# Two norms in a row: the second one's factor taken behind the projections it feeds

## The reference, cut to what matters

```python
h = layer_norm(DEEPNORM_ALPHA * h + swiglu_ffn(h, ...), ln_ffn_g[1], ln_ffn_b[1])   # end of the first block
...
h = rms_norm(x, norm_mix_g[0])        # x * rsqrt(mean(x * x) + 1e-6) * g
z = h @ w_in                          # even_mixer
u, v, q, k, vb = jnp.split(z, [512, 1024, 1536, 2048], axis=-1)
a_out = chunked_gmlp(jax.nn.gelu(u, approximate=False), jax.nn.gelu(v, approximate=False), ...)
qh, kh, vh = rms_norm(heads(q), q_g), rms_norm(heads(k), k_g), heads(vb)
```

## Time and profile before

| | |
|---|---|
| median of the runs | 2374.08 us |
| the profiled execution's own time | 2375.46 us |
| its span | 2373.8 us |
| PE busy | 2327.5 us (98%) |
| DVE busy | 1645.7 us (69%) |
| ACT busy | 1067.6 us (45%) |
| POOL busy | 326.8 us (14%) |
| the stretch of the change | 1232 to 1290 us of the span |

### The profile page before, as it was taken

The page is one execution under the profiler, slowest core; times in us unless marked ns, Lnnn a source line. Parts: engine busy times, 40 slices in busy tenths (PEclk is TensorE's granted clock), DMA queues, the critical chain, the costliest instruction groups (busy, mean ns, idle before and its releaser), DMA issues.

```text
span 2373.8 us, 36382 instructions
## 1 busy us (share of the span) xinstructions
PE 2327.5 (98%) x14683; PEld 2023.1 (85%) x14683; DVE 1645.7 (69%) x2191; ACT 1067.6 (45%) x1390; POOL 326.8 (14%) x295
## 2 busy tenths in 40 slices
PE   7799999999999999999999999999999999999999
PEld 7688899988886678999878779999887878899987
DVE  8835877746666778777486546999647655799942
ACT  6421544532336625446234453555523454455622
POOL 6402100002002340000123252000011002000000
PEclk9899999999999999999999999999999999999999
DMA  2432333233332123333333323332334212333332
GB/s 58 96 106 89 99 110 104 81 102 105 97 107 67 32 84 98 103 103 93 88 120 94 93 68 101 95 107 72 110 97 144 71 54 71 89 108 107 88 106 85
DMA packets 328908, 219.65 MB, mean 93 GB/s; under 512 B 11252, under 2 KB 319114, under 8 KB 328682
## 3 DMA queue, kind: packets, MB, share of 16 engines
q1 hardware_dynamic: 322362, 208.46, 29.7%
q0 software_dynamic: 3024, 7.90, 1.4%
q10 hardware_dynamic: 3360, 1.02, 0.2%
HBM read 206.59 MB, written 2.10 MB: 88 GB/s over the span
## 4 chain that ended last, share of the span: by engine, by line
PE 89%; DVE 5%; POOL 3%; ACT 2%; issue 1%; ACTq 0%; DMA 0%; SPq 0%; DVEq 0%; POOLq 0%
PE psum L1512 10%; PE psum L1514 10%; PE psum L1513 10%; PE psum L1259 9%; PE psum L1261 9%; PE psum L1260 9%; PE psum L1481 3%; PE psum L1482 3%; PE psum L1483 3%; PE psum L1680 1%; PE psum L1682 1%; PE psum L1681 1%; PE psum L1377 1%; PE psum L1373 1%; PE psum L1374 1%
## 5 line engine op out<-in xcount | busy, mean ns | idle before, releaser
L2272 ACT CAST w_hi<-w_stage 128x2048 fp32r<-128x2048 f32 x118 | 225.4, 1911 | 535.6 <-PE psum L1261 352.9
L3269 DVE TENSOR_TENSOR w_lo<-w_stage,w_hi 128x2048 fp32r<-128x2048 f32 x119 | 285.0, 2395 | 228.6 <-ACT w_hi L2272 228.5
L1512 PE MATMUL psum<-x_sum_hi,w_hi 128*128 128x256 f32 x1088 | 308.0, 283 | 0.0
L1513 PE MATMUL psum<-x_sum_lo,w_hi 128*128 128x256 f32 x1088 | 307.9, 283 | 0.0
L1514 PE MATMUL psum<-x_sum_hi,w_lo 128*128 128x256 f32 x1088 | 307.9, 283 | 0.0
L2342 ACT CAST w_hi<-w_parts 128x1024 fp32r<-128x1024 f32 x204 | 213.4, 1049 | 201.1 <-PE psum L1514 111.1
L3397 DVE TENSOR_TENSOR w_lo<-w_parts,w_hi 128x1024 fp32r<-128x1024 f32 x204 | 248.3, 1220 | 51.3 <-ACT w_hi L2342 50.1
L1259 PE MATMUL psum<-hidden_raw_hi,w_hi 128*128 128x512 f32 x594 | 232.1, 391 | 0.3 <-DVE w_lo L3269 0.3
L1261 PE MATMUL psum<-hidden_raw_hi,w_lo 128*128 128x512 f32 x594 | 231.1, 389 | 0.0
L1260 PE MATMUL psum<-hidden_raw_lo,w_hi 128*128 128x512 f32 x594 | 231.1, 389 | 0.0
L1512 PE MATMUL psum<-x_hi,w_hi 128*128 128x256 f32 x816 | 230.9, 283 | 0.0
(11 more groups left out here) (657 smaller groups left out, 5285.6 us busy)
## 6 DMA issues: line engine op xcount, KB each, us to landing
w_stage<-in_ffn_w_down_dram SPq DMA_DIRECT2D x64, 704.0 KB, 4.7
w_parts<-in_ffn_w_gu_dram SPq DMA_DIRECT2D x144, 256.0 KB, 3.5
w_parts<-in_ffn_w_gate_dram SPq DMA_DIRECT2D x64, 256.0 KB, 3.1
w_parts<-in_ffn_w_up_dram SPq DMA_DIRECT2D x64, 256.0 KB, 3.1
w_stage<-in_ev_w_in_dram SPq DMA_DIRECT2D x10, 1024.0 KB, 5.3
w_stage<-in_ssm_w_glu_dram SPq DMA_DIRECT2D x8, 1024.0 KB, 5.6
w_stage<-in_ffn_w_gu_dram SPq DMA_DIRECT2D x8, 1024.0 KB, 5.2
w_stage<-in_sb_w_qkv_dram SPq DMA_DIRECT2D x8, 1024.0 KB, 5.1
```

What stands on the lines that cost most here:

```text
L1512: nc.tensor.matmul(dst, hi, x_hi[:, k, :], start=(start and k == 0), stop=False, skip_group_check=True)
L1513: nc.tensor.matmul(dst, hi, x_lo[:, k, :], start=False, stop=False, skip_group_check=True)
L2272: nc.scalar.copy(whi[:, half, :], wst[:, half, :]).then_inc(whi_done, 1)
L3269: V.tensor_tensor(wlo[:, half, :], wst[:, half, :], whi[:, half, :].bitcast(F32), ALU.subtract).then_inc(wlo_done, 1)
```

## The change

The chunks that feed the projections now hold the layer norm's result times the second norm's gain, without the second factor. The last step on a chunk becomes a `tensor_scalar` that adds the bias, from SBUF to SBUF, where it was a `scalar_tensor_tensor` with bank 7 as second input. ACT copies the three sums out of banks 3, 2 and 0 into SBUF (`sums_kept`), and PE's first product of `ev_u` waits for the copies. The seven steps for the second mean square are written behind chunks 3 and 5, and ACT's two for the factor behind the rounding of chunk 6; the factor (`even_scale`) lies in SBUF. ACT's `rstd_keep` moves from behind chunk 1 to behind chunk 7. `keep_busy` shrinks from 25 products to 10.

The factor is then applied to the results. In `ev_u` DVE multiplies each bank in place (`ev_u_stage`), and only then does ACT's Gelu read it. PE transposes `even_scale` between banks 2 and 3, DVE copies the four columns out as `even_cols`, and a `memset` at the end of `ev_u_stage`, behind both weight splits, is what PE's `ev_v` waits for. In `ev_v` the Gelu takes `even_cols` as its scale, in `ev_qk` the evacuation multiplies by `even_scale` in place of 1.0, and in `ev_vb` it multiplies by `even_cols`.

```diff
--- before.py
+++ after.py
@@ -365,6 +365,8 @@
         gain_parts, gain_means = cols[:, 4 * DC:4 * DC + 3], cols[:, 4 * DC + 3:4 * DC + 6]
         rstd_one, rms_in, mean_keep, rstd_keep = bank[6], bank[4], sq[:, 0, :], sq[:, 0, :]
         part_in, cross_in = tmp_b[:, 0, :], sq[:, 1, :]
+        sums_kept = [at(f"gain_sums_kept{n}", [P, SEQ], hid_at + (60 + 2 * n) * KB)[:, :] for n in range(3)]
+        even_scale, even_cols = qk_rs[:, 7, :], stat[:, 96:96 + TT]
         z_slot = [tmp_a[:, 0, :], tmp_a[:, 1, :], tmp_c[:, 1, :]]
 
 
@@ -1378,6 +1380,8 @@
                                             stop=(k == DC - 1), skip_group_check=True)
 
                 every = slice(0, SEQ)
+                if n == 3:
+                    pe.wait_ge(ln_m2, 2 * 3 + 5)
                 pe.wait_ge(wlo_done, st.it0 * 2 + 1)
                 for h in range(2):
                     pe.wait_ge(ln_hi, n * LN_UNITS + h + 1)
@@ -1411,6 +1415,11 @@
                         high(b, k, every)
                         mm = low(b, k)
                     mm.then_inc(part_done, 1)
+                    if n == 3 and b == 2:
+                        pe.wait_ge(act_link, link_count(3) + 4)
+                        for t in range(TT):
+                            mm = nc.tensor.transpose(bank[7][:, t * P:(t + 1) * P], even_scale[:, t * P:(t + 1) * P], ident[:, :])
+                        mm.then_inc(ln_sums, 1)
 
             def keep_busy(count, b=3):
 
@@ -1637,7 +1646,7 @@
                 for b, m, what in ((3, 0, "first"), (2, 1, "squared"), (0, 2, "crossed")):
                     pe.wait_ge(dev_sq, dev_at[what, DC - 1])
                     nc.tensor.matmul(bank[b], ones_mean[:, :], gain_sums[:, m, :], start=True, stop=True).then_inc(ln_sums, 1)
-                keep_busy(25, 1)
+                keep_busy(10, 1)
 
             def mean_gains():
 
@@ -2131,6 +2140,7 @@
                 elif name == "ev_u":
                     feature_stage(name, xhi, xlo, lambda k: (x_ready, x_count(3) + k + 2), norm_in=3)
                 elif name == "ev_v":
+                    pe.wait_ge(ln_n, 4 * LN_UNITS + TT + 1)
                     token_stage(name, xhi, xlo)
                 elif name == "ev_qk":
                     feature_stage(name, xhi, xlo, lambda k: (x_ready, x_count(3) + k + 2), None,
@@ -2523,16 +2533,20 @@
                     act.wait_ge(ln_sums, sums_count(n) + 1)
                     nc.scalar.activation(mean_sq, mean, ACT.Square).then_inc(ln_m2, 1)
                     nc.scalar.copy(mean_keep, mean).then_inc(ln_m2, 1)
-                    rstd_of(0, slice(0, SEQ), rstd_one)
-                    act.wait_ge(ln_var, 2 * n + 2)
-                    nc.scalar.activation(sq[:, 1, :], rms_in, ACT.Ln, bias=gain_means[:, 2:3]).then_inc(act_link, 1)
-                    act.wait_ge(act_link, link_count(n) + 3)
-                    nc.scalar.activation(bank[7], sq[:, 1, :], ACT.Exp, scale=-0.5).then_inc(act_link, 1)
+                    for m, of in enumerate((3, 2, 0)):
+                        if m == 1:
+                            rstd_of(0, slice(0, SEQ), rstd_one)
+                        act.wait_ge(ln_sums, sums_count(n) + 3 + m)
+                        nc.scalar.copy(sums_kept[m], bank[of]).then_inc(ln_m2, 1)
                     for m, (c, tokens) in enumerate(ln_units):
                         act.wait_ge(ln_n, n * LN_UNITS + m + 1)
                         nc.scalar.copy(xhi[:, c, tokens], z_slot[c % 3][:, tokens]).then_inc(ln_hi, 1)
-                        if c == 1:
-                            nc.scalar.activation(rstd_keep, rstd_ln, ACT.Exp, scale=-0.5).then_inc(ln_m2, 1)
+                        if c == 6:
+                            act.wait_ge(ln_var, 2 * n + 2)
+                            nc.scalar.activation(sq[:, 1, :], rms_in, ACT.Ln, bias=gain_means[:, 2:3]).then_inc(act_link, 1)
+                            act.wait_ge(act_link, link_count(n) + 3)
+                            nc.scalar.activation(even_scale, sq[:, 1, :], ACT.Exp, scale=-0.5).then_inc(act_link, 1)
+                    nc.scalar.activation(rstd_keep, rstd_ln, ACT.Exp, scale=-0.5).then_inc(ln_m2, 1)
                     return
 
                 for h in range(2):
@@ -2773,7 +2787,7 @@
                     for half in range(2):
                         for u in range(2):
                             n = 2 * half + u
-                            act.wait_ge(part_done, i * 4 + (st.part0 + n + 1))
+                            act.wait_ge(ln_n, 4 * LN_UNITS + n + 1)
                             nc.scalar.activation(dst[:, bass.ds(i * 4 + n, 1), :], bank[n].unsqueeze(1), func).then_inc(evac_done, 1)
                         split_next(half)
                 stage_loop(name, body)
@@ -2783,7 +2797,7 @@
                 split(st.it0 + 1, 0, st.part0 + TT)
                 for n in range(TT):
                     act.wait_ge(part_done, st.part0 + TT + n + 1)
-                    nc.scalar.activation(dst[:, n, :], bank[4 + n], func).then_inc(evac_done, 1)
+                    nc.scalar.activation(dst[:, n, :], bank[4 + n], func, scale=even_cols[:, n:n + 1]).then_inc(evac_done, 1)
                 split(st.it0 + 1, 1, st.part1)
 
             def even_tables():
@@ -3762,34 +3776,58 @@
                 dve.wait_ge(ln_sums, sums + 2)
                 V.tensor_tensor(variance, bank[6], mean_sq, ALU.subtract).then_inc(ln_var, 1)
 
-                dve.wait_ge(ln_m2, 2 * 3 + 2)
-                dve.wait_ge(ln_sums, sums + 3)
-                link(V.tensor_tensor(part_in, mean_keep, bank[3], ALU.mult))
-                dve.wait_ge(ln_sums, sums + 4)
-                link(V.scalar_tensor_tensor(rms_in, part_in, -2.0, bank[2], ALU.mult, ALU.add))
-                link(V.scalar_tensor_tensor(part_in, mean_sq, gain_means[:, 0:1], rms_in, ALU.mult, ALU.add))
-                dve.wait_ge(act_link, link_count(3) + 2)
-                link(V.tensor_tensor(rms_in, part_in, rstd_one, ALU.mult))
-                dve.wait_ge(ln_sums, sums + 5)
-                link(V.scalar_tensor_tensor(cross_in, mean_keep, gain_means[:, 1:2], bank[0], ALU.mult, ALU.add))
-                link(V.scalar_tensor_tensor(part_in, cross_in, 2.0, rms_in, ALU.mult, ALU.add))
-                V.tensor_tensor(rms_in, part_in, rstd_one, ALU.mult).then_inc(ln_var, 1)
-
-                for c in range(DC):
+                def centre(c):
+                    V.tensor_tensor(res[:, c, :], res[:, c, :], mean, ALU.subtract).then_inc(ln_xc, 1)
+
+                def weighted(c):
                     z = z_slot[c % 3]
-                    V.tensor_tensor(res[:, c, :], res[:, c, :], mean, ALU.subtract).then_inc(ln_xc, 1)
                     dve.wait_ge(ln_xc, xc_count(3) + c + 1)
                     if c >= 3:
                         dve.wait_ge(x_ready, x_count(3) + c - 3 + 2)
-                    link(V.scalar_tensor_tensor(z, res[:, c, :], gain_rms[:, c:c + 1], rstd_one, ALU.mult, ALU.mult))
-                    dve.wait_ge(act_link, link_count(3) + 4)
                     for tokens in TOKEN_HALVES if c == 0 else (slice(0, SEQ),):
-                        V.scalar_tensor_tensor(z[:, tokens], z[:, tokens], bias_rms[:, c:c + 1], bank[7][:, tokens], ALU.add,
-                                               ALU.mult).then_inc(ln_n, 1)
+                        link(V.scalar_tensor_tensor(z[:, tokens], res[:, c, tokens], gain_rms[:, c:c + 1], rstd_one[:, tokens],
+                                                    ALU.mult, ALU.mult))
+                        V.tensor_scalar(z[:, tokens], z[:, tokens], bias_rms[:, c:c + 1], 0.0, ALU.add, ALU.add).then_inc(ln_n, 1)
+
+                first, squared, crossed = sums_kept
+                dve.wait_ge(ln_m2, 2 * 3 + 2)
+                centre(0)
+                centre(1)
+                dve.wait_ge(act_link, link_count(3) + 2)
+                weighted(0)
+                weighted(1)
+                for c in range(2, DC):
+                    centre(c)
+                    weighted(c)
+                    if c == 3:
+                        dve.wait_ge(ln_m2, 2 * 3 + 5)
+                        link(V.tensor_tensor(part_in, mean_keep, first, ALU.mult))
+                        link(V.scalar_tensor_tensor(rms_in, part_in, -2.0, squared, ALU.mult, ALU.add))
+                        link(V.scalar_tensor_tensor(part_in, mean_sq, gain_means[:, 0:1], rms_in, ALU.mult, ALU.add))
+                    if c == 5:
+                        link(V.tensor_tensor(rms_in, part_in, rstd_one, ALU.mult))
+                        link(V.scalar_tensor_tensor(cross_in, mean_keep, gain_means[:, 1:2], crossed, ALU.mult, ALU.add))
+                        link(V.scalar_tensor_tensor(part_in, cross_in, 2.0, rms_in, ALU.mult, ALU.add))
+                        V.tensor_tensor(rms_in, part_in, rstd_one, ALU.mult).then_inc(ln_var, 1)
+
+            def ev_u_stage():
+
+                st = ST["ev_u"]
+                dve.wait_ge(act_link, link_count(3) + 4)
+                for half in range(2):
```

(30 more changed lines are left out.)

## The result

The changed kernel took 2383.48 us, the median of six runs (2382.28 to 2387.15), against 2374.11 for the kernel before (six runs, 2371.61 to 2376.03): a ratio of 1.0044, 95% interval 1.0034 to 1.0054. It is slower by about 9.4 us; 2386 was forecast, in a range from 2379.5 to 2391.

The account below looks back on a forecast made before the run. PE was taken as the bound, a late start of `ev_v` delaying the end one for one. Front and chunks 2.3, seam 6.8 and clock 2.4 gave 11.5 us, with the tail 12: 2386, range 2379.5 to 2391.

Parts of the forecast that it names:

- The front: Start of `ev_u`: 4.1 us early unhindered, but POOL's `w_lo` holds the first bias step, so PE starts 3.1 us early.
- The supply of chunks: Chunks in `ev_u`: 2.34 us each beside POOL, plus the moved steps on DVE; banks 0 and 1 done 2.3 us later.
- The seam: From banks 0 and 1 to `ev_v`: PE waits for the mark behind both weight splits, 12.3 against 5.5, costing 6.8 us.
- The clock: Restart of `ev_v`: PE's clock falls once, behind about six idle us, costing 2.4 us.
- The sum: Whole kernel: 9.1 + 2.4 = 11.5 us later, with a little for the tail 12, giving 2386.
- The downstream edits: Scaling in `ev_qk`, `ev_v` and `ev_vb`: claimed to cost nothing; with the other small items, +-0.5 us together.
- (1) No lock: DVE and POOL run side by side in `ev_u`: +5.1 us, with the slow restart +7.5, 2381; chance 18%.
- (2) The clock falls inside `ev_u`: PE's clock falls already there and stays low into `ev_v`: +15.5 us, 2389.5; chance 20%.
- (3) The early start carrying through: In `ev_u` chunks keep up with PE's early start and only the seam costs: 2375.5, not slower; chance 8%.
- (4) The mark not holding PE: At `ev_v` the mark is passed before the second split; the seam costs 1 us, time 2372 to 2378; chance 4%.

Follow-up runs that it names:

- e2: Changed kernel with the gain step writing PSUM bank 7 and the bias step reading it from there; 2383.28 us.
- e4: Changed kernel with all seven steps for the second mean square, and ACT's two, moved behind chunk 7; 2384.66 us.
- e1: Changed kernel with the mark that lets PE into `ev_v` put ahead of the second weight split; 2377.41 us.
- e3: Changed kernel with 27 small products on PE between `ev_u` and its wait for the mark; 2382.48 us.
- f1: e4 plus half 0's cast and split earlier, transposes behind bank 3, mark before the second split and awaited only before `ev_v`'s fourth tile; 2371.21 us.
- f2: f1 with the bias step reading PSUM bank 7, as in e2; 2369.32 us, ratio 0.9983 to the kernel before.

## Why the prediction was right

**The front.** PE was to start near 5.6 us behind the start of the variance, at 1242.1 on the clock of before; measured 5.60. The cause is the one named: POOL's `w_lo` held the first bias step, 1.84 us, and e2 took that away.

**The supply of chunks.** Forecast 2.34 us a chunk beside POOL, measured 2.31 (L3790 at 1241.66 and, for chunk 3, 1243.97); the blocked step was forecast to end 0.29 behind POOL and did; the steps cost two stretches of DVE, and PE's gaps were 2.13 and less. Banks 0 and 1 were forecast 2.3 us late and were 2.0. Chunk 7 was in fact 0.6 sooner than forecast (`x_lo` there at 27.49, forecast 28.07), and the clock took some of it back: PE, at its lower level for chunk 6, came to `x_lo` of chunk 7 0.36 us after it was there, where it had been 0.05 before. e4 shows that the steps make the gaps: with them elsewhere, banks 0 and 1 are done 4.0 us sooner.

**The seam.** Forecast 12.3 us from banks 0 and 1 to `ev_v` against 5.5; measured 12.32 (40.62 - 28.30) against 5.49. e1 shows the cause: one mark moved, 6.1 us back. That the number fits to 0.02 is partly luck: half way, at the end of the first split, the chain was 0.34 us behind the forecast (6.09 against 5.75), and the shorter steps from there on made it up.

**The clock.** Forecast 2.4; measured eight products at 0.43 in place of 0.227, 1.7 us. e3 shows that the mechanism is right. The size is not fixed: the clock stayed low for 3.6 us behind the restart here, for 5.3 in e2 and 5.7 in e4, which cost 1.7, 2.4 and 2.7 us by the start of the 25th product (against e3). So 2.4 was in the middle of what these three traces show, and the profiled execution of the changed kernel is at the low end.

**The sum.** 8.84 + 1.7 = 10.5 us at the seam by the traces; 12 forecast, of which 0.5 was a rounding up that nothing stood behind; 9.4 by the medians, 8 to 13 by the interval. The three errors (0.3 at banks 0 and 1, 0.7 in the clock, 0.5 of rounding) all point the same way, so none hid another. The downstream edits cost nothing visible: behind the restart the two traces are 6.9 us apart (5.18 at `ev_v`'s first product, and 1.7), and their spans differ by 6.8.

**The rivals.** (1) No lock: refuted by 0.49 against 0.89 beside POOL, and by e2. (2) The clock falls inside `ev_u`: it did, behind the gaps of chunks 5 and 6, though the prediction counted nothing for it. But it was back at its upper level before banks 2 and 3, so the 3 us of this rival did not come, only the 0.3 above, and 0.6 more in e1 and e3. Some delay there is free, as the prediction said: bank 3 was ready at 1267.26 and DVE came to it at 1267.97. (3) The early start carrying through: the pitch was under 2.72 as its condition asked, but the four steps in one piece at chunk 5 broke it. (4) The mark not holding PE: refuted by the row with 6.23.

The Trainium skill, page "SBUF — State Buffer", section "Who interferes with whom", has a VectorE instruction with two SBUF inputs contend with a GpSimd instruction that reads SBUF. The trace agrees, though the other way round than I had put it into the range: L3805 began at 1245.50, 0.1 before `x_lo`, and it was POOL that took 1.75 in place of 1.29. Three of the moved steps have both inputs in SBUF (L3804, L3805 and L3809), not the two that the prediction counts. L3805 and L3809 met POOL, DVE had begun first both times, and none was lengthened; what one costs that begins inside a POOL instruction, no run shows.

## What to carry to other kernels

Moving work off the path to a first start pays only if the place it is moved to is not the bound: here it was moved in between the chunks that the same engine had to supply. When a scale is taken behind a product, look at what else the evacuation was in front of; the splits of the next weights stood behind it, and a release mark written as the last line of a stage made PE wait for all of them. And when work is moved behind the last chunk, see what else stands there: in e4 it pushed a table load onto the path. Put a mark directly behind the instruction whose result it guards (in e1 that alone took two thirds of the loss back), and wait for it at the first use, as in f1. With the steps moved behind the last chunk, the next cast and split ahead of the factor, and the bias step in PSUM as well (f2), the same idea turned from 9 us slower to some 4 us faster.

## What the runs showed of the hardware

A DVE `tensor_scalar` with a column as its scalar over 512 fp32 columns took 0.49 us from SBUF to SBUF alone, 0.89 where POOL was in the middle of its own instruction (it ended 0.29 behind POOL's each time), and 0.75 from PSUM in any company; the pass from PSUM with constants took 0.69. So the quick form is the slow one beside POOL, and PSUM a refuge. PE's clock fell after gaps of 0.68 and 2.13 us with few products between them; the single gap of 0.90 us at 1238.47 had left it up, and so did the 1.40 us ahead of `ev_v` in e1. Behind idle times of 6.23, 5.92 (e2) and 9.78 us (e4) it took 3.6, 5.3 and 5.7 us of products to come back.
